# Layer 1 projection in split products of three passes, with resident high and low weights and compact key pairs

## The reference

```
x = layer_norm(ALPHA * x + ffn, ln2_g[0], ln2_b[0])
q, k, v = split(x @ c_w_in, [1024, 1280])      # 16 query, 4 key, 4 value heads of 64
q = rms_norm(q, c_q_norm); k = rms_norm(k, c_k_norm)
q, k = rope(q, row and column angles), rope(k, ...)   # halves of each head
softmax(q k^T / 8) v @ c_w_out
```

## Time and profile before

| | us |
|---|---|
| median of 3 runs (lowest, highest) | 3824.79 (3821.1, 3826.29) |
| profiled execution, its own time | 3822.31 |
| its span | 3820.3 |
| TensorE matmul busy | 3390.0 (89%) |
| VectorE busy | 2566.9 (67%) |
| ScalarE busy | 2023.9 (53%) |
| GpSimd busy | 349.4 (9%) |
| mean granted TensorE clock | 0.949 of full speed |

### The profile page before, as it was taken

How to read it: one execution, slowest core, us unless ns; L and a number is a source line. 1 busy time by engine, 2 the same in 40 slices (tenths; PEclk the granted TensorE clock), 3 DMA queues, 4 the chain that set the end, 5 groups by cost and what they waited for, 6 DMA issues and landing times. The chain is left out here.

```text
span 3820.3 us, 52025 instructions
## 1 busy us (share of the span) xinstructions
PE 3390.0 (89%) x18712; PEld 2729.3 (71%) x18712; DVE 2566.9 (67%) x3961; ACT 2023.9 (53%) x2800; POOL 349.4 (9%) x300
## 2 busy tenths in 40 slices
PE   9985669579999999987996899998939999999993
PEld 7873348479999999973453456556839999999993
DVE  2678965667667667644664778885567667666665
ACT  3116743246666666641334778883225666665664
POOL 0000000011111111101110000000010111111102
PEclk9998889789999999998997999999969999999996
DMA  3110213458777777734211110003247778778774
GB/s 121 37 37 26 64 40 115 144 194 260 251 236 255 252 234 256 244 105 154 81 77 58 37 34 22 22 17 117 110 169 250 239 245 260 238 247 260 237 232 151
DMA packets 359940, 585.36 MB, mean 153 GB/s; under 512 B 17440, under 2 KB 283680, under 8 KB 358304
## 3 DMA queue, kind: packets, MB, share of 16 engines
q1 hardware_dynamic: 335136, 489.67, 38.1%
q0 software_dynamic: 14336, 50.34, 5.9%
q10 hardware_dynamic: 10368, 44.04, 2.8%
HBM read 505.36 MB, written 78.64 MB: 153 GB/s over the span
## 5 line engine op out<-in xcount | busy, mean ns | idle before, releaser
L1123 PE MATMUL h_ps<-xT,high 128*128 128x384 f32 x3584 | 1063.8, 359 | 2.7 <-DVE xT L1245 2.7
L1241 DVE TENSOR_TENSOR low<-raw,high 128x2048 fp32r<-128x2048 f32 x384 | 877.2, 2285 | 147.9 <-ACT high L1185 147.9
L1124 PE MATMUL h_ps<-xT,low 128*128 128x192 f32 x3584 | 904.4, 252 | 0.0
L1185 ACT ACTIVATE high<-raw 128x2048 fp32r<-128x2048 f32 x384 | 733.1, 1910 | 283.3 <-PE yp_ps L1156 176.1
L1124 PEld LDWEIGHTS h_ps<-xT,low 128*128 128x128 f32 x3584 | 683.3, 191 | 1.3
L1123 PEld LDWEIGHTS h_ps<-xT,high 128*128 128x128 f32 x3584 | 674.3, 188 | 4.7 <-issue 3.2
L1312 DVE TENSOR_TENSOR gate_up<-h_ps,cross 128x384 f32<-128x384 f32 x256 | 142.8, 558 | 306.3 <-ACT cross L1204 306.3
L1204 ACT ACTIVATE cross<-h_ps 128x384 f32<-128x384 f32 x256 | 125.6, 491 | 278.8 <-PE h_ps L1127 278.7
L1448 PE MATMUL qkv_ps<-w_in,xT 128*128 128x512 f32 x576 | 255.4, 600 | 8.9 <-ACT xT L1468 6.9
L1708 DVE TENSOR_REDUCE col<-s_ps 128x1 f32<-128x1024 f32 (+1 forms) x192 | 200.5, 1044 | 78.9 <-PE s_ps L1663 78.4
L195 DVE SCALAR_TENSOR_TENSOR cat<-glu,taps,cat 128x264 f32<-128x264 f32 (+28 forms) x412 | 248.0, 671 | 0.0
(11 more groups left out here) (238 smaller groups left out, 5824.3 us busy)
## 6 DMA issues: line engine op xcount, KB each, us to landing
raw<-moe_w_gate SPq DMA_DIRECT2D x128, 1024.0 KB, 5.2
raw<-moe_w_up SPq DMA_DIRECT2D x128, 1024.0 KB, 7.7
raw<-moe_w_down SPq DMA_DIRECT2D x128, 1024.0 KB, 6.9
rows_x<-x ACTq DMA_DIRECT2D x36, 512.0 KB, 2.6
rows_acc<-ax ACTq DMA_DIRECT2D x24, 512.0 KB, 2.9
r<-rows_acc SPq DMA_DIRECT2D x24, 512.0 KB, 8.0
rows_qT_parts<-qT ACTq DMA_DIRECT2D x12, 1024.0 KB, 3.9
q<-rows_qT_parts SPq DMA_DIRECT2D x24, 512.0 KB, 3.6
```

What stands on the lines that cost most here:

```text
L1123: nc.tensor.matmul(ps, wh[:, n, k, :], xT[:, u, k, :, :].rearrange("p s n -> p (s n)"), start=(k == 0), stop=False)
L1124: nc.tensor.matmul(ps[:, 0:SLOTS], wl[:, n, k, :], xT[:, u, k, 0, :], start=False, stop=False)
L1185: nc.scalar.activation(split_view(high, at), piece_view(at), ACT.Copy).then_inc(high_ready, 1)
L1241: nc.vector.tensor_tensor(split_view(low, at), piece_view(at), split_view(high, at).bitcast(F32), ALU.subtract).then_inc(low_ready, 1)
```

## The change

`project_axial` is rewritten without loops. The weights come through four buffers of one row block each, and are kept as a high and a low part, both resident. Tile 0's products follow the weights, row block by row block; later tiles go chunk by chunk, and ScalarE takes each chunk as it is done. The layer norm works in place in r, with two fused passes. x is turned from r and split into high and low on its way out of PSUM. The rotary tables are loaded per tile and multiplied by the norm weights (queries and keys apart), so the separate multiply by the norm weights goes and cosine and sine multiplies are done in two pieces each. Keys are stored twice, (high, low), as queries are: 20 blocks in two batches of 10. The turned q has one buffer instead of two. SP now issues the stores of x2 and of q as well as all loads. `axial_attention` first makes the missing halves of the keys: for the first group by copies, for the second by three transfers from SBUF to SBUF. The diff, cut to its core:

```diff
 def project_axial(...):
             @block.sync
+                load_r(0)
                 sp.dma_start(gain[:], ...); sp.dma_start(shift[:], ...)
...
+                load_r(1)
+                for k in range(KD):
+                    if k >= SLOTS_W:
+                        sp.wait_ge(w_low, k - SLOTS_W + 1)
+                    sp.dma_start(raw[k % SLOTS_W][:], m["c_w_in"][0][k * P:(k + 1) * P, :]).then_inc(w_in[k], 16)
+                    if k == 1:
...
+                        store_x2(0)
+                        store_x2(1)
+                for t in range(TILES + 2):
+                    if 0 < t < TILES - 1:
+                        store_x2(t + 1)
+                    if t >= 2:
+                        sp.wait_ge(qT_ready, 2 * (t - 2) + 2)
+                        sp.dma_start(m["qT_parts"][(t - 2) * P:(t - 1) * P, :], qT[:].bitcast(F32)).then_inc(q_out, 16)
+                    if t < TILES - 2:
+                        sp.wait_ge(xT_done, t + 1)
+                        sp.wait_ge(x2_out, 16 * (t + 2 if t else 2))
+                        load_r(t + 2)
+                    if 1 <= t < TILES - 1:
+                        sp.wait_ge(rotated, t)
+                        load_rope(t + 1)
+                sp.wait_ge(q_out, 16 * TILES)
...
             @block.tensor
+                def product(t, k, n):
+                    for at, (one, other) in enumerate(((xh, wh), (xh, wl), (xl, wh))):
+                        last = nc.tensor.matmul(qkv_ps[:, to], one[:, t % 2, cols], other[:, k, to], ...)
...
+                for k in range(KD):
+                    pe.wait_ge(w_low, k + 1)
+                    for n in range(CHUNKS):
+                        last = product(0, k, n)
...
+                turn_x(1)
+                for t in range(1, TILES + 2):
+                    if t >= 2:
+                        turn_qk(t - 2, 0)
+                    if t < TILES:
+                        pe.wait_ge(xl_ready, t + 1)
+                        chunk(t, 0)
+                    if t >= 2:
+                        turn_qk(t - 2, 1)
+                    if t + 1 < TILES:
+                        turn_x(t + 1)
+                    if t < TILES:
+                        chunk(t, 1)
+                        chunk(t, 2)
             @block.scalar
+                for t in range(TILES + 2):
+                    if t >= 2:
+                        copy_q(t - 2, 0)
+                    if t < TILES:
+                        copy_chunk(t, 0)
+                    if t >= 2:
+                        copy_q(t - 2, 1)
+                    if t + 1 < TILES:
+                        high_x(t + 1)
+                    if t < TILES:
+                        copy_chunk(t, 1)
+                    if 1 <= t <= TILES:
+                        high(t - 1)
+                    if t < TILES:
+                        copy_chunk(t, 2)
+                        square(t)
             @block.vector
+                def stats_of(t):
+                    v.wait_ge(r_in[t % 2], 16 * (t // 2 + 1))
...
+                for t in range(2):
+                    stats_of(t)
+                    apply(t)
+                low_x(0)
+                for k in range(KD):
+                    v.wait_ge(w_high, k + 1)
+                    nc.vector.tensor_tensor(wl[:, k, :], raw[k % SLOTS_W][:], wh[:, k, :].bitcast(F32), ALU.subtract).then_inc(w_low, 1)
...
+                for t in range(TILES + 1):
+                    if t + 2 < TILES:
+                        stats_of(t + 2)
+                    if t:
+                        mean_square(t - 1)
+                    if t + 2 < TILES:
+                        apply(t + 2)
+                    if t:
+                        rotate(t - 1)
+                    if t + 1 < TILES:
+                        low_x(t + 1)
+                    if t:
+                        low(t - 1)
 def axial_attention(...):
             @block.sync
+                for to in range(2):
+                    sp.dma_start(group(to, 1, 1).bitcast(F32), group(1, 1, 0).bitcast(F32)).then_inc(spread_in, 16)
                 with sp.Fori(0, GROUP_TILES[0]) as t:
                     load(t)
+                sp.wait_ge(spread_in, 32)
+                sp.dma_start(group(1, 1, 0).bitcast(F32), group(0, 1, 0).bitcast(F32)).then_inc(spread_in, 16)
             @block.vector
+                def spread(g):
+                    nc.vector.tensor_copy(group(1, g, 1), group(1, g, 0).bitcast(F32)).then_inc(low_down, 1)
+                    v.wait_ge(low_down, g + 1)
+                    v.wait_ge(low_up, g + 1)
+                    nc.vector.tensor_copy(group(1, g, 0), group(0, g, 0).bitcast(F32)).then_inc(keys_ready, 1)
```

More of the change, by code:

```diff
@@ L1331, in _, with project_axial @@
                 pairs_of(v, pair)
-def project_axial(c, m, keys, values):
+def project_axial(c, m, keys, values, under_keys, under_picks):
     nc = c.nc
@@ L1360, in project_axial @@
[L1360 to L1365, removed]
+        under_qk = next_address(nc)
@@ L1367, in project_axial, with heads @@
             c.sem(n) for n in ("rotated", "high_ready", "parts_ready", "qkT_done", "qT_ready"))
[L1368 to L1372, removed]
+        by_head = parts[:].rearrange("p (h s d) -> p h s d", s=2, d=DH)
+        pairs = ((0, 0, AX_H), (1, AX_H, HEADS))
+        def heads(t):
+            return qk[:, t % 2, :].rearrange("p (h d) -> p h d", d=DH)
@@ L1387, in _ @@
-                load(Tile(0, 0))
-                load(Tile(0, 1))
-                sp.dma_start(rope[:], m["rope_c"].rearrange("(t p) n -> p t n", p=P)).then_inc(rope_in, 16)
-                for k in range(KD):
[L1391 to L1397, removed]
+                sp.dma_start(ident[:], m["ident"]).then_inc(ident_in, 16)
@@ L1435, in turn_qk @@
                     last.then_inc(qkT_done, 1)
[L1437 to L1455, removed]
@@ L1457, in _ @@
-                pe.wait_ge(tables_in, 80)
-                turn_x(Tile(0, 0))
-                tile_steps(pe.Fori(0, turns - 2), step)
+                def product(t, k, n):
+                    cols, to = slice(k * P, (k + 1) * P), slice(n * HALF, (n + 1) * HALF)
+                    for at, (one, other) in enumerate(((xh, wh), (xh, wl), (xl, wh))):
+                        last = nc.tensor.matmul(qkv_ps[:, to], one[:, t % 2, cols], other[:, k, to], start=(k == 0 and at == 0), stop=(k == KD - 1 and at == 2))
+                    return last
@@ L1476, in square @@
[L1476 to L1486, removed]
@@ L1502, in step @@
[L1502 to L1505, removed]
-                    if rotary:
-                        high(a.next(-1))
-                    if products:
-                        copy_qkv(a)
-                    if following:
-                        copy_x(a.next())
-                    if products:
-                        square(a)
-                act.sem_inc(copied, 1)
@@ new lines, in square, with high @@
+                def square(t):
+                    act.wait_ge(copied, CHUNKS * (t + 1))
+                    if t:
+                        act.wait_ge(rotated, t)
+                    nc.scalar.activation(ra[:].rearrange("p h d -> p (h d)"), qk[:, t % 2, :], ACT.Square).then_inc(squared, 1)
+                def high(t):
+                    act.wait_ge(rotated, t + 1)
+                    if t:
+                        act.wait_ge(qkT_done, 2 * t)
+                    nc.scalar.activation(by_head[:, :, 0, :], heads(t), ACT.Copy).then_inc(high_ready, 1)
@@ L1529, in _ @@
                 s = Steps(v, dve)
-                heads = qk[:].rearrange("p (h d) -> p h d", d=DH)
-                def norm(a):
-                    v.wait_ge(r_in[a.slot], a.pair * 16 + 16)
-                    v.wait_ge(x2_out[a.slot], a.pair * 16 + 16)
-                    v.wait_ge(xT_done, a.t + 1)
-                    layer_norm_rows(nc, s, r[:, a.slot, :], x2[:, a.slot, :], stats, mv, gain[:], shift[:], var_ready, rstd_ready, a.t).then_inc(x2_ready, 1)
-                def rotate(a):
-                    v.wait_ge(squared, a.t + 1)
-                    v.wait_ge(rope_in, 16)
+                def stats_of(t):
+                    row, mean = r[:, t % 2, :], mv[:, t % 2, :]
+                    v.wait_ge(r_in[t % 2], 16 * (t // 2 + 1))
+                    for h in range(2):
+                        s.add(nc.vector.bn_stats(stats[:, 6 * h:6 * h + 6], row[:, h * HALF:(h + 1) * HALF]))
+                    s.settle()
+                    s.link(nc.vector.bn_aggr(mean[:, 0:2], stats[:]))
+                    nc.vector.tensor_scalar(mean[:, 2:3], mean[:, 1:2], LN_EPS, None, ALU.add).then_inc(var_ready, 1)
@@ L1556, in rotate @@
-                    s.settle()
-                    nc.vector.tensor_tensor(heads, ra[:], rb[:], ALU.add).then_inc(rotated, 1)
-                    v.wait_ge(high_ready, a.t + 1)
-                    nc.vector.tensor_tensor(q_parts[:, :, 1, :], heads[:, 0:AX_H, :], q_parts[:, :, 0, :].bitcast(F32), ALU.subtract)
-                    for n in range(2):
```

(32 more changed lines are left out.)

203 lines of the change are left out of this document (130 added, 73 removed).

## The result

The changed kernel takes 3896.43 us (median of 4 runs, 3894.61 to 3897.03), the kernel before beside it 3823.45: 1.0186 times as long, 95% interval 1.0174 to 1.0199. The forecast was 3884 us, its range 3846 to 3915.

What follows compares the result with a forecast made beforehand. TensorE bounds the old kernel at 24.8 us per tile; the change closes a loop through r's load, 33.5 us per round. Stage +51.7 and attention head +7.5 give about +59 us: 3884 us, range 3846 to 3915.

Steps and rivals of the forecast that it cites:

- start, to turn(0, 0): Stage start: tile 0 ends earlier, first turn at about 1780 instead of 1787.2; -7 us (bounds -14 and 0).
- rounds 2 to 9: The eight rounds that load r(t+2): period 33.5 us instead of 24.8, together +70 us.
- round 10, round 11: Rounds without an r load: round 10 TensorE-bound with a cold start, -2.7 us; round 11 without x to turn, -4.8.
- attention's head: Start of layer 1 attention: two 1 MB SBUF transfers stand ahead of q on SP; +7.5 us (bounds +3 and +11).
- The closed loop: Each tile: r's load waits for q's store, VectorE for r, TensorE for VectorE; 31.3 us, 33.5 with the clock.
- the path to the store's issue: In the loop: first turn, chunk 0, second turn and ScalarE's copies until q's store is issued; 9.45 us before clock loss.
- the store's issue to r: In the loop: r lands behind q's 1 MB store on one queue, 5.1 us after store issue (bounds 3.7 and 7.2).
- sum and root: In the loop: VectorE's reduce, GpSimd's root, first multiply, 5.34 us; layer norm passes lie under the 3.65 us root wait.
- The clock: After 11.4 us idle each round, TensorE's burst starts at 1.2 GHz, losing 2.2 us (bounds 1.5 and 7.9).
- mild loop: Rival: clock holds and r lands 3.7 us after the issue; period 29.9 us, total 3853 us; chance 0.10.
- loop at the low clock: Rival: bursts too short to restore the clock before the second turn, 5.7 us more per round, 3930 us; chance 0.05.
- TensorE as the bound: Rival: r arrives before VectorE asks, ten rounds save 4.9 us each; -52 us, 3772 us; chance 0.09.

Runs made afterwards that it cites:

- e1: Changed kernel with SP's load of r(t+2) put ahead of the wait for and store of tile t-2's turned q: 3790.65 us, ratio 0.9903.
- e2: Changed kernel with the wait for and store of the turned q moved from SP to ScalarE's queue: 3790.19 us, ratio 0.9899.
- e7: Changed kernel with SP loading r(t+2) first, behind no current-round work, q stored by ScalarE, a semaphore per x2 buffer: 3775.23 us, ratio 0.9869.
- e3: Changed kernel with only the high by high pass of the projection, both passes with a low part left out: 3859.23 us, ratio 1.0079.
- e5: Changed kernel with VectorE's two layer norm passes moved from beside GpSimd's root to the end of its tile list: 3900.53 us, ratio 1.0188.
- e4: Changed kernel with 48 unread FP32R matmuls added at the end of TensorE's work in rounds 2 to 9: 3893.75 us, ratio 1.0177.
- e6: Changed kernel with the attention's first two q loads ahead of the two 1 MB transfers between SBUF partitions: 3886.61 us, ratio 1.0149.

## Why the prediction was right

The direction and the mechanism held; the size was 14 us short, within the range. The forecast added 59 us, the kernel took 73 us more. By its steps, in us against the kernel before, from the stage's first DMA on:

| step | forecast | measured |
|---|---|---|
| start, to turn(0, 0) | -7 | -4.0 |
| rounds 2 to 9 | +70 | +75.5 |
| round 10, round 11 | -2.7, -4.8 | -3.8, -5.2 |
| last tile, its turns | -2.7, -1.1 | -2.9, -1.3 |
| attention's head | +7.5 | +11.8 |
| sum | +59 | +70 |

Of the 3 to 4 us that the table leaves, 2.5 lie ahead of the stage, where nothing was edited: its first DMA comes at 1718.29 before and at 1720.78 after, and between 1717 and 1723 in the other runs.

- **The closed loop** (under "What it waits for instead") is shown by e1, e2 and e7: take r's load out from behind the store of q, and 34.2 us become 21.3 (e1, on average) or 19.5 (e7). e3 shows that of TensorE's products only chunk 0 is in it.
- **Its terms.** Of the 34.28 us (forecast 33.5), the path to the store's issue took 10.77 (forecast 9.45 and 2.2 for the clock), the store's issue to r 6.2 (forecast 5.15), statistics 1.64, sum and root 6.30 (forecast 5.34), rotate 6.52, high and low 2.85. That the round came out within 0.8 us is in part luck: the path's term, 0.9 too high, hid nearly half of the two that were 2.0 too low. The root was mis-sized: 4.51 us, not the 3.54 of before, since VectorE's two passes over r, put into its shadow, run beside it (e5). r behind a store of 1 MB took 1 us longer than the rate of the earlier trace rows gave: in these rounds r landed 5.6 us after its issue (median; 3.3 before) and the store of q 4.8 (3.9 before).
- **The clock.** It fell in every round, as said; the cost was 1.5 us (8.16 between the turns, against 6.6 at 2.4 GHz in e4 and e7), the low bound, not 2.2. The text let each term stand alone. e5 shows that they need not add: while the clock falls once a round, a term cut elsewhere can come back as a longer spell at 1.2 GHz. In e3 it did not: 3.5 us less between the turns made the round 3.6 us shorter.
- **The start** gained 4.0 us, not 7: the first turn (1785.72) waited 4.5 us for low parts, and VectorE had waited 4.8 us for r(3), whose load went out at 1765.17, behind the store of x2(2) at 1762.48.
- **The attention's head** was the other size that was off, 0.8 us above its upper bound of +11: the matmul that waits for q starts 14.4 us after its issue at 2130.48, with 2 MB of transfers over 64 partitions ahead of it, which landed 9.5 us after issue (median). The windows of 4 us from 2129 to 2141 show 176 to 196 GB/s, below the 246 of the earlier trace rows.
- **The rivals.** The mild loop did not come: the clock fell, and r took 6.2 us from the store's issue, not 3.7. The loop at the low clock did not either: the clock was back at 2.4 GHz 3.1 us after the restart. TensorE as the bound did not come, but its condition, r ahead of VectorE's demand, is e7's edit, and then it came at 19.5 us per round, 19.9 forecast.

## What to carry to other kernels

An instruction list that issues both the stores of one round's results and the loads for a later round can close a loop through every engine between them: write down, for each load, which round's work it stands behind, and put it ahead of all waits of the current round. Price a faster engine by what is on the loop (here one chunk of three), not by its busy time. Where the clock falls in each round, a saving of a microsecond elsewhere can vanish, as in e5; opening the loop, so that the idle gap itself goes, was what paid here (e1, e7).

## What was not expected of the hardware

- GpSimd's power over 128 x 20 took 4.51 us beside VectorE's passes with two tensor inputs and 3.54 us beside small ones (e5); the layer norm's root over one column took 1.5 us beside such a pass, in the changed kernel's start, instead of 0.55.
- Gaps of 2.1 to 2.8 us in otherwise dense work were followed by a spell at 1.2 GHz in six of eight cases in e4 and, at 2.4 and 2.6 us, in both of e1; after gaps of 1.2 to 1.5 us the clock stayed at 2.4 GHz in all four of e1. Length is not all: ahead of tile 0's first turn a gap of 3.1 us was followed by the low clock in e6 (9.4 us to the second turn) and not in e1 (6.6).
- Casts of 64 x 2048 FP32 took 1.22 us on VectorE and 1.91 us on ScalarE, so the keys' three copies were done by 2131.7, 3.4 us after the stage's first issue, where 4.5 were forecast.
